# Weight sums of a seven-product FFN pair, made by adding DMA transfers, and the pair one step later

## The chip, the cores and the metric

The program runs on one core of one Trainium2 chip. The metric is the device time of one execution in microseconds (us); lower is better. TensorE (PE) multiplies, VectorE (DVE), ScalarE (ACT) and GpSimd (POOL) work on tiles in SBUF and PSUM, and SyncE (SP) issues DMA transfers. GpSimd has a DMA queue of its own.

## The reference, cut to what matters

The network works on x of 256 tokens by 1024. Around its mixers it has five feed-forward networks (FFNs), each with hidden width 2816, in float32:

```
x = x + 0.5 * swiglu(rms_norm(x, ffn1_norm_g[i]), ffn1_w_in[i], ffn1_w_out[i])

def swiglu(x, w_in, w_out):
    gate, up = jnp.split(x @ w_in, 2, axis=-1)
    return (jax.nn.silu(gate) * up) @ w_out
```

The fifth has its weights in three matrices (gate, up, down). The change touches these FFNs alone.

## The kernel before, in words

**Precision.** Each float32 operand of a product is split into a rounded part and a rest (hi and lo), and a product is three matmuls: hi by hi, hi by lo, lo by hi. For the weights ACT makes w_hi from w_raw (round_, L803) and DVE makes w_lo (split, L1412).

**Units.** The weights stream in units of 128 x 2048 float32 (1.05 MB) through a ring of three buffers. SP loads unit u when DVE has split unit u-3. PE takes a unit in 24 matmuls of 512 columns. All engines walk the same list of units.

**An FFN** has 11 steps (NI = 11), of 256 hidden columns each. G(i,0) and G(i,1) are the gate and up weights of step i for the two halves of the 1024 inputs, D(i) its down weights. PE's order is G(i,0), G(i,1), D(i-1). The hidden tile of step i goes the following way: ACT's silu and DVE's product make h_s (L895, L1527), GpSimd cuts it into 16-bit words (cut, L750), SP transposes it by DMA (turn_back, L528), GpSimd joins the words (join, L754), ACT makes y_hi (L899), DVE makes y_lo (hidden_low, L1532), and PE uses both in D(i).

**The pair.** At steps PAIR = 7 and 8 the two steps together are a 2 x 2 block product (two token halves, two input halves, two column groups). It is done with seven block products (Winograd's form of Strassen's method) and not eight, so that a pair has three units of G and four sums T1 to T4 of weight blocks in place of four units. A block product is 12 matmuls. For it:

- SP loads the four raw blocks (block, L524), half a block at a time, two halves in each of steps 1 to 4.
- DVE makes the four T sums (t_sum, L1575) in steps 3, 4 and 5.
- GpSimd makes x_sum = xg_hi + xg_lo after join(1) (x_sums, L760) and the four S sums after join(2) (s_sums, L767 to L772).
- ACT makes the hi parts (L923, L928), DVE the rests (L1581, L1587), in steps 4 to 6 and in the pair.
- In the pair PE's blocks M1, M5, M6, M2, M3, M7, M4 follow each other, and ACT and DVE combine them (snap, C11, C12, C22, C21).

GpSimd works strictly in the order written: cut(i), join(i), and in between whatever stands there.

Of the kernel before, what the change touches and what calls it, by code (L numbers as in the profile page):

```python
# [25 lines left out]
P = 128  # L26
# [17 lines left out]
PAIR = 7  # L44


def gate_at(i, half):

    if i < PAIR + 2:
        return half if i == 0 else 3 * PAIR + 1 if i == PAIR + 1 else 3 * i - 1 + half  # L50
    return 3 * i - (3 if i == PAIR + 2 else 2) + half


def down_at(i):

    if i == NI - 1:
        return 3 * NI - 2
    return 3 * i + (4 if i < PAIR - 1 else 5 if i < PAIR + 1 else 3)

# [18 lines left out]
def plan_units():  # L78

    first, opens = {}, []  # L80

    def add(name, pattern):
        first[name] = len(opens)
        opens.extend(c == "g" for c in pattern)

    ffn = "d" * (3 * NI - 1)
    add("mem", "dddd")
    add("ffn0", ffn)
    add("mixa", "ggggg" + "d" * 10)
    add("mixa_out", "d" * (A_OUT // 256))  # L90
    add("ffn1", ffn)
    add("ffn2", ffn)
    add("mixb", "d" * 7)
    add("mixb_out", "d" * (A_OUT // 256))
    add("ffn3", ffn)
# [11 lines left out]
    add("ffn4", ffn)  # L107
    return first, opens


def build(nc, a, out, known=None):
# [6 lines left out]
    with ExitStack() as ctx:  # L118
# [97 lines left out]
        t_landed = [sem(f"t_landed{k}") for k in range(4)]  # L216
        ffn_cut, ffn_back, ffn_joined = (sem(n) for n in ("ffn_cut", "ffn_back", "ffn_joined"))
# [92 lines left out]
        def bank(u):  # L310

            return 4 + (u + sum(u > U[f"ffn{f}"] + 3 * NI - 2 for f in range(5))) % RING
# [33 lines left out]
        T1, T3, T2, T4 = range(4)  # L346
        x_sum = tiles(KB(40, 8))
# [139 lines left out]
        def _(sp):  # L487
# [23 lines left out]
            def ffn(f):  # L511
                u = U[f"ffn{f}"]

                def gate_up(half, i):
                    load(u + gate_at(i, half), gu_src(f, half, i), split_cols=True)

                def down(i):
                    load(u + down_at(i), down_src(f, i))

                def block(k, half):  # L520

                    j, part = half, gu_src(f, *((0, PAIR), (0, PAIR + 1), (1, PAIR + 1), (1, PAIR))[k])[half]
                    dst = t_raw[k].rearrange("p (k c) -> p k c", k=4)[:, :, 256 * j:256 * j + 256]
                    sp.dma_start(dst, part).then_inc(t_landed[k], 16)  # L524

                def turn_back(i):
                    sp.wait_ge(ffn_cut, 2 * ((NI - 1) * nth[f] + i) + 2)
                    sp.dma_start_transpose(out=h_back, in_=h_sent).then_inc(ffn_back, 16)  # L528

# [5 lines left out]
                for i in range(1, PAIR):  # L535
                    gate_up(1, i)
                    down(i - 1)
                    if i == 1:
                        sp.wait_ge(w_used, u + 1)
                    if i < 5:  # L540
                        block(i - 1, 0)
                    gate_up(0, i + 1)
                    turn_back(i - 1)
                    if i < 5:
                        block(i - 1, 1)
                gate_up(1, PAIR)
                gate_up(1, PAIR + 1)
                down(PAIR - 1)
                turn_back(PAIR - 1)
                gate_up(0, PAIR + 2)  # L550
                gate_up(1, PAIR + 2)
                down(PAIR)
                down(PAIR + 1)
                turn_back(PAIR)
                if PAIR + 3 < NI:
                    gate_up(0, PAIR + 3)
                turn_back(PAIR + 1)
                for i in range(PAIR + 3, NI):
                    gate_up(1, i)
                    down(i - 1)  # L560
                    if i < NI - 1:
                        gate_up(0, i + 1)
                    turn_back(i - 1)
                down(NI - 1)
# [117 lines left out]
        def _(pool):  # L682
# [61 lines left out]
            def ffn(f):  # L744
# [18 lines left out]
                def s_sums():  # L763
                    a11, a12, a21, a22 = (x_sum[:, 4 * h:4 * h + 4, P * tt:P * tt + P] for tt in range(2) for h in range(2))
                    s1, s2, s3, s4 = (tiles(s_raw[:, j], P) for j in range(4))
                    pool.wait_ge(pool_done, pool_.at(f"X {f} 6"))
                    pool.tensor_tensor(s1, a21, a22, ALU.add).then_inc(pool_done, pool_(f"S1 {f}"))  # L767
                    pool.tensor_tensor(s3, a11, a21, ALU.subtract).then_inc(pool_done, pool_(f"S3 {f}"))
                    pool.wait_ge(pool_done, pool_.at(f"S1 {f}"))
                    pool.tensor_tensor(s2, s1, a11, ALU.subtract).then_inc(pool_done, pool_(f"S2 {f}"))  # L770
                    pool.wait_ge(pool_done, pool_.at(f"S2 {f}"))
                    pool.tensor_tensor(s4, a12, s2, ALU.subtract).then_inc(pool_done, pool_(f"S4 {f}"))  # L772
# [3 lines left out]
                for i in range(1, NI - 1):  # L776
                    cut(i)
                    pool.wait_ge(ffn_hl, NI * nth[f] + i)
                    join(i)
                    if i == 1:  # L780
                        x_sums()
                    if i == 2:
                        s_sums()
# [9 lines left out]
        def _(act):  # L793
# [72 lines left out]
            def ffn(f, n, gain):  # L866
                u = U[f"ffn{f}"]
# [19 lines left out]
                def silu(i, tt, src=None):  # L887
                    if src is None:
                        if tt == 0:
                            act.wait_ge(ffn_gu, (NI - 2) * nth[f] + (i + 1 if i < PAIR else i - 1))  # L890
                        else:
                            act.wait_ge(w_used, u + gate_at(i, 1) + 1)
                    if i and i + NI * nth[f]:
# [7 lines left out]
                def step(i, last=False):  # L901
                    v = u + gate_at(i, 0)
                    round_(v + 2)
                    hidden_high(i - 1, (i - 1) % 2)
                    if i == 4:
                        t_high(T1, f"T1 {f}")
                    if i == 5:
# [4 lines left out]
                    if i == 5:  # L912
                        t_high(T2, f"T2 {f}")
                    round_(v + 4)
                    if last:
                        act.wait_ge(ffn_ht, nth[f] + 1)
                        act.activation(y_hi[:, 2 * (i % 2):2 * (i % 2) + 2], tiles(ps[:, 6, :]), ACT.Copy).then_inc(ffn_hh, 1)

                def t_high(k, made):
                    act.wait_ge(vec_done, vec.at(made))  # L920
                    if k == T2:
                        act.wait_ge(pool_done, pool_.at(f"S4 {f}"))
                    act.activation(t_hi[k], t_raw[k], ACT.Copy).then_inc(act_done, act_(f"T hi {f} {k}"))  # L923

                def s_high():
                    act.wait_ge(pool_done, pool_.at(f"S4 {f}"))
# [3 lines left out]
                def taken(k, bank_):  # L930
# [2184 lines left out]
```

## Time and profile before

| what | us |
|---|---|
| runs of the kernel | 1535.16, 1537.32, 1537.65 (median 1537.32) |
| the profiled execution, its own time | 1531.57 |
| its span, first to last instruction | 1529.8 |
| PE busy in it | 1517.7 |
| DVE busy | 1094.3 |
| ACT busy | 858.6 |
| POOL busy | 358.5 |

The profile is one execution. Busy time is that in which an engine executes anything; an engine's idle time matters only where PE has to wait for it. Ends of matmuls are modelled, so waits of PE are best read from the starts of neighbouring matmuls. The mean granted clock of PE was 0.999 of full speed.

### The profile page before, as it was taken

Reading aid. Unit: us, or ns where it says so; the run is one execution under the profiler, and the core shown is the slowest. Engines: PE = TensorE matmul, PEld = TensorE weight load, DVE = VectorE, ACT = ScalarE, POOL = GpSimd, SP = SyncE. Lnnn points to the kernel's source line nnn. Section 1 sums busy time; section 2 is a strip of 40 time slices with the busy share of each in tenths; the row PEclk is TensorE's granted clock in tenths of the full one; section 3 lists DMA queues with packets and bytes.
Section 4 is the critical chain, followed back from the end, with each engine's and each line's share of the span. In section 5 each row is a group of like instructions: output and inputs, shape, how many; then the busy total and the mean of one; then the engine's idle time right before and its main releaser. Section 6 shows DMA issues by size and latency. Waiting matters only on the chain.

```text
span 1529.8 us, 19935 instructions
## 1 busy us (share of the span) xinstructions
PE 1517.7 (99%) x7906; PEld 1292.2 (84%) x7906; DVE 1094.3 (72%) x1174; ACT 858.6 (56%) x1075; POOL 358.5 (23%) x256
## 2 busy tenths in 40 slices
PE   9999999999999999999999999999999999999998
PEld 7888888888778888888888888899988899888886
DVE  6677766557778567776776678599998566666875
ACT  7545554645365454556776456476887343464554
POOL 0352200001732135320001631100571000017320
PEclk9999999999999999999999999999999999999999
DMA  7977665457776688765416986766554665578763
GB/s 253 314 243 233 188 182 188 138 170 211 239 246 192 193 275 251 228 195 173 158 56 206 285 230 203 209 191 204 181 181 147 212 192 187 173 223 273 226 194 102
DMA packets 274309, 311.43 MB, mean 204 GB/s; under 512 B 64272, under 2 KB 233512, under 8 KB 274216
## 3 DMA queue, kind: packets, MB, share of 16 engines
q1 hardware_dynamic: 273112, 308.84, 64.4%
q8 instruction: 63, 1.03, 0.3%
q10 hardware_dynamic: 1104, 1.31, 0.3%
q14 instruction: 30, 0.25, 0.0%
HBM read 295.92 MB, written 1.09 MB: 194 GB/s over the span
## 4 chain that ended last, share of the span: by engine, by line
PE 90%; POOL 3%; DVE 2%; issue 2%; DMA 2%; ACT 2%; ACTq 0%; DVEq 0%; POOLq 0%
PE ps L2344 22%; PE ps L2348 22%; PE ps L2345 22%; PE ps L2334 3%; PE ps L2336 3%; PE ps L2335 3%; PE ps L2546 2%; PE ps L2545 2%; PE ps L2544 2%; DMA scr<-scr 1%; PE ps L2387 1%; PE ps L2500 1%; POOL scr L750 1%; DVE w_lo L1412 1%; POOL scr L760 0%
## 5 line engine op out<-in xcount | busy, mean ns | idle before, releaser
L1412 DVE TENSOR_TENSOR w_lo<-w_raw,w_hi 128x2048 fp32r<-128x2048 f32 x250 | 598.5, 2400 | 185.1 <-ACT w_hi L803 184.7
L803 ACT ACTIVATE w_hi<-w_raw 128x2048 fp32r<-128x2048 f32 x250 | 477.0, 1912 | 250.8 <-PE ps L2348 200.5
L2344 PE MATMUL ps<-w_hi,xg_hi 128*128 128x512 f32 (+1 forms) x960 | 375.2, 391 | 1.2 <-DVE scr L1527 1.2
L2348 PE MATMUL ps<-w_hi,xg_lo 128*128 128x512 f32 (+1 forms) x960 | 372.1, 388 | 0.0
L2345 PE MATMUL ps<-w_lo,xg_hi 128*128 128x512 f32 (+1 forms) x960 | 372.0, 387 | 0.0
L750 POOL COPY scr<-scr 128x512 uint16<-128x512 uint16 x100 | 121.1, 1231 | 697.8 <-DVE scr L1527 697.7
L2344 PE MATMUL ps<-w_hi,y_hi 128*128 128x512 f32 x666 | 261.9, 393 | 1.3 <-DVE y_lo L1532 0.7
L2348 PE MATMUL ps<-w_hi,y_lo 128*128 128x512 f32 x666 | 259.1, 389 | 0.0
L2345 PE MATMUL ps<-w_lo,y_hi 128*128 128x512 f32 x666 | 258.9, 389 | 0.0
L2344 PEld LDWEIGHTS ps<-w_hi,xg_hi 128*128 128x128 f32 x960 | 180.3, 188 | 39.1 <-DVE w_lo L1412 1.6
L2348 PEld LDWEIGHTS ps<-w_hi,xg_lo 128*128 128x128 f32 x960 | 180.3, 188 | 36.8
L2345 PEld LDWEIGHTS ps<-w_lo,xg_hi 128*128 128x128 f32 x960 | 180.4, 188 | 36.3
L2334 PE MATMUL ps<-xg_hi,w_hi 128*128 128x256 f32 x544 | 155.1, 285 | 0.0
L2336 PE MATMUL ps<-xg_hi,w_lo 128*128 128x256 f32 x544 | 153.9, 283 | 0.0
L2335 PE MATMUL ps<-xg_lo,w_hi 128*128 128x256 f32 x544 | 153.9, 283 | 0.0
L2344 PEld LDWEIGHTS ps<-w_hi,y_hi 128*128 128x128 f32 x666 | 125.1, 188 | 28.7 <-issue 1.8
L2348 PEld LDWEIGHTS ps<-w_hi,y_lo 128*128 128x128 f32 x666 | 125.0, 188 | 26.1
L2345 PEld LDWEIGHTS ps<-w_lo,y_hi 128*128 128x128 f32 x666 | 125.2, 188 | 24.9
L754 POOL COPY scr<-scr 128x1024 uint16<-128x1024 uint16 x50 | 82.2, 1645 | 200.7 <-DMA scr<-scr 200.7
L899 ACT ACTIVATE y_hi<-scr 128x512 fp32r<-128x512 f32 x50 | 31.4, 629 | 155.0 <-POOL scr L754 154.9
L2334 PEld LDWEIGHTS ps<-xg_hi,w_hi 128*128 128x128 f32 x544 | 104.4, 192 | 0.4 <-issue 0.3
L2335 PEld LDWEIGHTS ps<-xg_lo,w_hi 128*128 128x128 f32 x544 | 104.4, 192 | 0.0
(403 smaller groups left out, 1710.8 us busy)
## 6 DMA issues: line engine op xcount, KB each, us to landing
w_raw<-in_ffn_w_in_dram SPq DMA_DIRECT2D x168, 512.0 KB, 5.0
w_raw<-in_ffn_w_out_dram SPq DMA_DIRECT2D x88, 512.0 KB, 5.5
w_raw<-in_w_in_dram SPq DMA_DIRECT2D x82, 512.0 KB, 4.6
w_raw<-in_a_w_in_dram SPq DMA_DIRECT2D x28, 512.0 KB, 4.5
w_raw<-in_w_down_dram SPq DMA_DIRECT2D x22, 512.0 KB, 5.1
w_raw<-in_w_gate_dram SPq DMA_DIRECT2D x21, 512.0 KB, 4.1
w_raw<-in_w_up_dram SPq DMA_DIRECT2D x21, 512.0 KB, 5.2
y_raw<-in_ffn_w_in_dram SPq DMA_DIRECT2D x16, 512.0 KB, 5.4
```

Source lines behind the costliest of these rows:

```text
L750: pool.tensor_copy(h_words[:, :, tt::2], h_s[:, tt].bitcast(U16).rearrange("p (b c w) -> p w b c", w=2, c=P)).then_inc(ffn_cut, 1)
L754: pool.tensor_copy(KB(20, 2).bitcast(U16).rearrange("p (b t w) -> p w b t", w=2, t=P), h_back.rearrange("p (w b) t -> p w b t", w=2)).then ...
L803: act.activation(w_hi[:, u % RING, :], w_raw[:, u % RING, :], ACT.Copy).then_inc(w_rounded, 1)
L899: act.activation(y_hi[:, 2 * p:2 * p + 2], h_t, ACT.Copy).then_inc(ffn_hh, 1)
L1412: dve.tensor_tensor(w_lo[:, s, :], w_raw[:, s, :], w_hi[:, s, :].bitcast(F32), ALU.subtract).then_inc(w_split, 1)
L2334: pe.matmul(dst, hi, xh, start=start, stop=False, skip_group_check=True)
L2335: pe.matmul(dst, hi, xl, start=False, stop=False, skip_group_check=True)
L2336: last = pe.matmul(dst, lo, xh, start=False, stop=stop, skip_group_check=True)
L2344: pe.matmul(dst, xh, hi, start=start, stop=False, skip_group_check=True)
L2345: pe.matmul(dst, xh, lo, start=False, stop=False, skip_group_check=True)
L2348: return pe.matmul(dst, xl, hi, start=False, stop=stop, skip_group_check=True)
L2544: pe.matmul(ps[:, bank_, :], xh[:, k], hi[:, c], start=start and k == 0, stop=False, skip_group_check=True)
```

## The change: what it does

- **T sums.** DVE's four subtractions go. GpSimd issues four DMA transfers, SBUF to SBUF, that add the source to what stands in the destination (add). The form of the seven products is turned so that only sums, and no differences, of weight blocks are needed: T1 += T3, T3 += T2, T2 += T1, T4 += T2. The signs move to S1 and S4 and to U2 and C22. Each transfer waits on GpSimd for the ones that it builds on.
- **Where they stand.** With p = 8 (the pair), add(T1) comes between cut(5) and join(5), add(T3) after join(5), add(T2) between cut(6) and join(6), add(T4) after join(6).
- **Sums of x.** x_sum and the S sums are made by DVE in step 5 and no longer by GpSimd in steps 1 and 2; x_sum is one instruction in place of four.
- **The pair** is at steps 8 and 9, in all five FFNs. The places of units come from a list (ffn_places), which has room for more pairs; here each FFN has one.
- **Raw blocks.** SP loads them in step 5 (T1, T3, T2) and step 6 (T4) and not in steps 1 to 4.
- **hi parts and rests.** ACT's s_high is in step 6, T1 and T2 in step 7; DVE's rests of S are in step 6, of T1 in step 7, of T2 at the head of the pair. The rest of T1 waits for add(T2), that of T2 for add(T4), since these transfers read what the rest overwrites.
- **The last hidden tile** is handled in the pair, as step 10 is now the step that follows it.

```diff
-PAIR = 7
+PAIRS_OF = ((8,), (8,), (8,), (8,), (8,))
+
+def ffn_places(pairs):
+
+    order, i = [("G", 0, 0), ("G", 0, 1)], 1
+    while i < NI:
+        if i in pairs:
+            order += [("G", i, 0), ("G", i, 1), ("G", i + 1, 1), ("D", i - 1), ("G", i + 2, 0), ("G", i + 2, 1), ("D", i), ("D", i + 1)]
+            i += 3
+        else:
+            order += [("G", i, 0), ("G", i, 1), ("D", i - 1)]
+            i += 1
+    return {step: k for k, step in enumerate(order + [("D", NI - 1)])}
...
@@ SyncE, step i (p is the pair)
+                    if i == p - 3:
+                        block(p, 0, 0)
+                        block(p, 0, 1)
+                    gate_up(1, i)
+                    if i == p - 3:
+                        block(p, 1, 0)
+                        block(p, 1, 1)
+                    down(i - 1)
+                    if i == p - 2:
+                        block(p, 3, 0)
+                    if i < NI - 1:
+                        gate_up(0, i + 1)
+                    turn_back(i - 1)
+                    if i == p - 3:
+                        block(p, 2, 0)
+                        block(p, 2, 1)
+                    if i == p - 2:
+                        block(p, 3, 1)
...
@@ GpSimd
-                def x_sums():
-                    pool.wait_ge(xl_ready, 8 * (norm_of[f"ffn{f}"][0] + 1))
-                    for k in range(0, 8, 2):
-                        pool.tensor_tensor(x_sum[:, k:k + 2], xg_hi[:, k:k + 2].bitcast(F32), xg_lo[:, k:k + 2].bitcast(F32),
-                                           ALU.add).then_inc(pool_done, pool_(f"X {f} {k}"))
...
+                def add(p, k, src):
+
+                    n = pair_count(f, p)
+                    if k in (T1, T3, T4):
+                        pool.wait_ge(t_landed[k], 32 * n)
+                    pool.wait_ge(*{T1: (t_landed[T3], 32 * n), T3: (t_landed[T2], 32 * n), T2: (t_added[T1], 16 * n), T4: (t_added[T2], 16 * n)}[k])
+                    if k == T3:
+                        pool.wait_ge(t_added[T1], 16 * n)
+                    if k == T2:
+                        pool.wait_ge(t_added[T3], 16 * n)
+                    pool.dma_start(t_raw[k], t_raw[src], accum_op=ALU.add).then_inc(t_added[k], 16)
...
                 for i in range(1, NI - 1):
                     cut(i)
+                    if i + 3 == pairs[0]:
+                        add(i + 3, T1, T3)
+                    if i + 2 == pairs[0]:
+                        add(i + 2, T2, T1)
...
                     pool.wait_ge(ffn_hl, NI * nth[f] + i)
                     join(i)
-                    if i == 1:
-                        x_sums()
-                    if i == 2:
-                        s_sums()
+                    if i + 3 == pairs[0]:
+                        add(i + 3, T3, T2)
+                    if i + 2 == pairs[0]:
+                        add(i + 2, T4, T2)
...
@@ VectorE, step i
-                    if i == 3:
-                        t_sum(T1, T3, T1, "T1")
-                    if i == 4:
-                        t_sum(T3, T2, T3, "T3")
-                    if i == 5:
-                        t_sum(T4, T4, T2, "T4")
-                    if i == 6:
-                        t_low(T2)
+                    if i == pairs[0] - 3:
+                        x_sums()
+                    if i + 2 == pairs[0]:
+                        s_lows((0, 1))
+                    if i + 1 in pairs:
+                        t_low(i + 1, T1)
                     split(v + 3)
...
+                    if i == pairs[0] - 3:
+                        s_sums()
+                    if i + 2 == pairs[0]:
+                        s_lows((2, 3))
                     split(v + 4)
...
+                def x_sums():
+
+                    dve.tensor_tensor(x_sum, xg_hi[:, :, :].bitcast(F32), xg_lo[:, :, :].bitcast(F32), ALU.add).then_inc(vec_done, vec(f"X {f}"))
...
+                def t_low(p, k):
+
+                    dve.wait_ge(act_done, act_.at(f"T hi {f} {p} {k}"))
+                    if k in (T1, T2):
+                        dve.wait_ge(t_added[T2 if k == T1 else T4], 16 * pair_count(f, p))
+                    dve.tensor_tensor(t_lo[k], t_raw[k], t_hi[k].bitcast(F32), ALU.subtract).then_inc(vec_done, vec(f"T lo {f} {p} {k}"))
...
+                def pair(p):
+
+                    n = u + at["G", p, 0]
+                    t_low(p, T2)
                     split(n + 2)
```

## Rows read from the trace of the kernel before

**Rows 1.** The page, part 1: busy us, share of the span, instructions.
```profile
PE 1517.7 (99%) x7906; PEld 1292.2 (84%) x7906; DVE 1094.3 (72%) x1174; ACT 858.6 (56%) x1075; POOL 358.5 (23%) x256
```

**Rows 2.** The waits, of PE: total us, times, longest us.
```profile
PE ps L2344 <- DVE scr L1527: 1.2, 1, 1.2
PE ps L2344 <- DVE y_lo L1532: 0.7, 1, 0.7
```

**Rows 3.** The windows, FFN 1 and FFN 2: stretch, its us, busy by engine.
```profile
372.00:522.00 150.00, 148.04 (x650) 121.43 (x649) 112.00 (x86) 76.00 (x71) 57.05 (x35) 1.00 0.76 233
522.00:701.00 179.00, 179.00 (x800) 148.26 (x799) 125.15 (x97) 94.84 (x93) 57.89 (x38) 1.00 0.73 226
```

**Rows 4.** The timeline of PE in FFN 1: start, us, instruction, idle before.
```profile
410.24 0.39 PE L2348 MATMUL ps<-w_hi,y_lo 128*128 128x512 f32 x1
411.87 0.47 PE L2344 MATMUL ps<-w_hi,xg_hi 128*128 128x512 f32 x1 [1.24 <-DVE scr L1527]
...
422.61 0.39 PE L2348 MATMUL ps<-w_hi,xg_lo 128*128 128x512 f32 x1
423.72 0.50 PE L2344 MATMUL ps<-w_hi,y_hi 128*128 128x512 f32 x1 [0.72 <-DVE y_lo L1532]
```

**Rows 5.** The timeline of POOL in FFN 1: first and last of four S sums, cuts.
```profile
400.88 3.31 POOL L767 TENSOR_TENSOR scr<-scr 128x512 f32<-128x512 f32 x1
...
409.26 3.22 POOL L772 TENSOR_TENSOR scr<-scr 128x512 f32<-128x512 f32 x1
412.43 5.30 POOL L750 COPY scr<-scr 128x512 uint16<-128x512 uint16 x2
```

**Rows 6.** The timeline of DVE in FFN 1, beside rows 5.
```profile
402.96 1.78 DVE L1532 TENSOR_TENSOR y_lo<-scr,y_hi 128x512 fp32r<-128x512 f32 x1
404.66 3.37 DVE L1575 TENSOR_TENSOR y_raw<-y_raw 128x2048 f32<-128x2048 f32 x1
407.95 3.38 DVE L1412 TENSOR_TENSOR w_lo<-w_raw,w_hi 128x2048 fp32r<-128x2048 f32 x1
```

**Rows 7.** The timeline of DVE in FFN 2, step 6.
```profile
632.27 0.69 DVE L1532 TENSOR_TENSOR y_lo<-scr,y_hi 128x512 fp32r<-128x512 f32 x1 [1.90 <-ACT y_hi L899]
632.89 2.28 DVE L1581 TENSOR_TENSOR scr_r<-scr,scr_r 128x2048 fp32r<-128x2048 f32 x1
635.09 2.28 DVE L1412 TENSOR_TENSOR w_lo<-w_raw,w_hi 128x2048 fp32r<-128x2048 f32 x1
```

**Rows 8.** The groups of instructions: count, busy us, mean ns of one.
```profile
L803 ACT ACTIVATE w_hi<-w_raw 128x2048 fp32r<-128x2048 f32 x250 | 477.0, 1912 | 250.8 <-PE ps L2348 200.5 <-PE ps L2336 40.0 <-DMA w_raw<-in_ffn_w_in_dram 7.6
...
L760 POOL TENSOR_TENSOR scr<-xg_hi,xg_lo 128x512 f32<-128x512 f32 x20 | 42.0, 2128 | 0.0
...
L1575 DVE TENSOR_TENSOR y_raw<-y_raw 128x2048 f32<-128x2048 f32 x5 | 16.9, 3377 | 0.0
...
L1575 DVE TENSOR_TENSOR scr<-scr 128x2048 f32<-128x2048 f32 x5 | 11.4, 2284 | 0.0
```

**Rows 9.** The timeline of PE in FFN 2: first matmul of D(5), of the pair.
```profile
635.96 0.39 PE L2344 MATMUL ps<-w_hi,y_hi 128*128 128x512 f32 x1
...
641.39 0.39 PE L2544 MATMUL ps<-w_hi,xg_hi 128*128 128x512 f32 x1
```

**Rows 10.** The timeline of SP in FFN 2: last raw half, turn_back(5).
```profile
596.35 0.58 SPq L524 DMA_DIRECT2D scr<-in_ffn_w_in_dram  x1
...
626.06 1.23 SPq L528 DMA_TRANSPOSE scr<-scr  x1
```

**Rows 11.** DMA issues: count, KB each, median us from issue to landing.
```profile
scr<-scr SPq DMA_TRANSPOSE x50, 3.1
...
scr<-mixer_rows SPq DMA_DIRECT2D x1, 512.0 KB, 3.6
```

**Rows 12.** The timeline of POOL in FFN 2: cut(5) and join(5).
```profile
622.80 3.23 POOL L750 COPY scr<-scr 128x512 uint16<-128x512 uint16 x2 [7.34 <-DVE scr L1527]
629.22 2.36 POOL L754 COPY scr<-scr 128x1024 uint16<-128x1024 uint16 x1 [3.18 <-DMA scr<-scr]
```

More of the change, by code:

```diff
@@ L346, in build, with pair_count, alone_until, alone @@
         T1, T3, T2, T4 = range(4)
+        def pair_count(f, p):
+            return sum(len(PAIRS_OF[g]) for g in range(f)) + PAIRS_OF[f].index(p) + 1
+        def alone_until(f, i):
+            def alone(f, j):
+                return j not in PAIRS_OF[f] and j - 1 not in PAIRS_OF[f]
+            return sum(alone(g, j) for g in range(f) for j in range(NI)) + sum(alone(f, j) for j in range(i + 1))
         x_sum = tiles(KB(40, 8))
@@ L534, in ffn @@
                     small_inputs()
-                for i in range(1, PAIR):
-                    gate_up(1, i)
-                    down(i - 1)
-                    if i == 1:
[L539 to L564, printed above, removed]
+                i = 1
+                while i < NI:
+                    if i in pairs:
+                        pair(i)
+                        i += 3
+                    else:
+                        step(i)
+                        i += 1
+                if NI - 3 not in pairs:
+                    down(NI - 1)
                 if f == 4:
@@ L911, in step @@
                         silu(i, tt)
-                    if i == 5:
-                        t_high(T2, f"T2 {f}")
+                    if i + 1 in pairs:
+                        t_high(i + 1, T2)
                     round_(v + 4)
[L915 to L923, printed above, removed]
+                    if i == NI - 1:
+                        last_hidden()
@@ L974, in ffn @@
                         act.activation(rope[:, j], rope[:, j], ACT.Sin).then_inc(act_done, act_(f"rope {j}"))
-                for i in range(3, PAIR):
-                    step(i)
-                pair()
-                for i in range(PAIR + 3, NI):
-                    step(i, last=i == NI - 1)
+                i = 3
+                while i < NI:
+                    if i in pairs:
+                        pair(i)
+                        i += 3
+                    else:
+                        step(i)
+                        i += 1
             def mem(n, gain):
@@ L1636, in ffn @@
                     pass
-                for i in range(3, PAIR):
-                    step(i)
-                pair()
-                for i in range(PAIR + 3, NI):
-                    step(i, last=i == NI - 1)
+                i = 3
+                while i < NI:
+                    if i in pairs:
+                        pair(i)
+                        i += 3
+                    else:
+                        step(i)
+                        i += 1
             def mem(n, gain, factor):
@@ L2588, in gates @@
+                    pe.wait_ge(vec_done, vec.at(f"C21 {f} {p}"))
+                    gates(p + 2)
+                    down(p)
+                    down(p + 1, hidden=(lambda: hidden(NI - 1)) if p + 2 == NI - 1 else None)
                 def gates(i, first=None):
-                    gate_up(u + gate_at(i, 0), 0, first=first)
-                    gate_up(u + gate_at(i, 1), 1)
-                for i in range(1, PAIR):
+                    gate_up(u + at["G", i, 0], 0, first=first)
+                    gate_up(u + at["G", i, 1], 1)
@@ L2594, in ffn, with step @@
+                def step(i):
                     gates(i, taken(i - 1))
@@ L2596, in ffn @@
                         pe.wait_ge(act_done, act_.at("M kT 1"))
-                    down(i - 1, start=i == 1)
-                pair()
-                for i in range(PAIR + 3, NI):
-                    gates(i, taken(i - 1))
-                    down(i - 1, hidden=(lambda: hidden(NI - 1)) if i == NI - 1 else None)
+                    down(i - 1, start=i == 1, hidden=(lambda: hidden(NI - 1)) if i == NI - 1 else None)
+                i = 1
+                while i < NI:
+                    if i in pairs:
+                        pair(i)
+                        i += 3
+                    else:
+                        step(i)
+                        i += 1
                 down(NI - 1, norm=n + 1)
```

283 lines of the change are left out of this document (152 added, 131 removed).

## The prediction

> **What bounds the kernel now.** I read the page first: TensorE (PE) is busy 1517.7 of 1529.8 us [rows 1]. The list of PE's waits has six entries, 4.8 us in all; two stand in the FFNs, 1.2 us on VectorE's (DVE's) h_s products and 0.7 us on its y_lo [rows 2]. The windows say where: the FFN stretches show PE busy all of their time but one, FFN 1, with 148.04 of 150.00 us [rows 3]. So neither the loads (DMA share about 0.75) nor DVE (125.15 of 179 us in FFN 2) binds; they only have to be in time. The change leaves PE's instructions as they are: seven products of 12 matmuls a pair, as before. All it can win is PE's waits, all it can lose is new ones.
>
> **The wait of FFN 1.** PE's timeline shows the two gaps [rows 4]. A unit is 24 matmuls, 641.39 - 635.96 = 5.43 us [rows 9], so a matmul follows its neighbour at 0.227 us. From 410.24 to 411.87 is 1.40 us too much, from 422.61 to 423.72 0.88: 2.3 us. Behind them stand GpSimd's S sums, 400.88 to 412.43, 11.6 us in one piece [rows 5]. The cuts of h_s are queued behind them and take 5.30 us (3.23 in FFN 2 [rows 12]), the transpose and the join follow them, and PE's down unit, the second gap, is late. DVE beside them needs 1.78 us for a y_lo of 0.69, 3.37 for the T1 sum and 3.38 for a split of 2.28 [rows 6, 7]; that split ends at 411.3, and PE goes on. The same sums are in the other FFNs, where 2 to 3 us of cover absorb them.
>
> The Trainium skill (SBUF — State Buffer, "Who interferes with whom") says the same of a DVE instruction with two SBUF inputs beside a GpSimd one that reads SBUF: one blocks the other. By that, moving sums off GpSimd makes both engines faster, and more than a count of instructions shows.
>
> **What is removed and added, per FFN.** GpSimd loses four x sums of 2128 ns and the S sums, 20 us in all [rows 5, 8]. DVE loses four T sums, 3.4 us the first, 2.3 the last of four [rows 8], about 10.4 us, and gains one x sum of 2048 elements (2.3 us by that last T sum) and four S sums of 512 elements (0.7 us each by y_lo [rows 7], 2.8): DVE minus 5 us. All of this is off PE. What it gives back is the 2.3 us of FFN 1, worth at most 0.15%. At pairs[0]-3 = step 5 DVE's new sums stand about where the T4 sum and T1's rest (2.5 us each) stood, so no new lateness there.
>
> The pair moves from steps 7, 8 to 8, 9: three more units in front, three fewer behind, PE's sum unchanged. The last hidden block now hangs in down(p+1) of the pair, with the same mid-unit transposes as step 10 had; down(8) now lies between gates(10) and it, so I cost it at 0.
>
> The T raw loads go from one block a step (steps 1 to 4) to three in step 5 and one in step 6. On SP's queue step 5 then puts block 0, G(5,1), block 1 and D(4) together, 4 x 1.05 MB. At 226 GB/s for a share of 0.73 the engines move 310 GB/s when busy [rows 3], so 3.4 us a megabyte. The four take 13.5 us from about 596.3, where FFN 2 issues its last raw half now [rows 10], so D(4) lands at about 610. PE takes D(5) at 635.96 [rows 9] and D(4) a step, 16.3 us, before: 619.6. ACT's rounding and DVE's split need 1.9 + 2.3 us before that [rows 7, 8], so 5 us of cover remain. Transposes turn_back(4) and (5) are issued after such bursts have drained. Cost 0.
>
> **The four adding transfers** decide. Each adds 1.05 MB of SBUF into SBUF from GpSimd's queue; before has no such operation. Bounds for one, call it L, to landing: a 0.5 MB transfer that ran by itself landed in 3.6 us [rows 11], of which 1.7 is data at 310 GB/s, so 1.9 us is fixed. One reading of 1.05 MB gives 3.4 + 1.9 = 5.3 us, the low end (no reason lets it be faster). Reading source and destination in turn gives 6.8 + 1.9 = 8.7. With half of the engines going to weight loads, 13.6 + 1.9 = 15.5, the high end. I take 8: two reads of long rows (8 KB a partition, where a weight row is 1 KB), mostly beside a weight load that has 12 us to spare.
>
> The Trainium skill (Collectives: The Full Stack, "The bandwidth ceiling") says that a DMA add costs two source reads on the reading side and so runs at half of a copy's rate. No row of before shows it. It speaks against the change: with it L is 8.7, not 5.3.
>
> Now the deadlines, with FFN 2's clock [rows 7, 9, 10, 12]. Steps are 16.3 us long, step 7 stays a step, the pair starts at 641.39 + 16.33 = 657.7.
> - T1's add is issued after cut(5), 622.80 + 3.23 = 626.0.
> - T3's waits for T1's and for join(5), 629.22 + 2.36 = 631.6: at 626 + L.
> - T2's waits for cut(6) (about 641) and T3's: max(641, 626 + 2L). join(6) is queued behind this wait.
> - T4's waits for T2's and join(6): 626 + 3L or 641 + L.
> - T2 is wanted by DVE's rest of T1, which needs 2.3 us, then a split of 2.3 [rows 7] before PE takes G(8,0) at 657.7: by 653.1, so L up to 9.0.
> - T4 is wanted by the rest of T2, which DVE now makes at the head of the pair, and PE's M6 two products later at 663.1: by 660.8, so 4L up to 34.8, L up to 8.7.
> - join(6) has to start by about 647 for D(6) at 652.3: L up to 10.5.
> At L = 8 nothing is late (T4 lands at 658). If the cover goes, each us of L over 8.7 costs 4 us a FFN, 20 us in the kernel.
>
> Sum: 2.3 us won, 0 lost. The profiled execution took 1531.57 us (span 1529.8), which would become 1529.3; the median of the three runs is 1537.3, 5.7 above it, and the result is compared with that. 1537.3 - 2.3 = **1535.0**.
>
> **Rivals.**
> *A, faster than can be overlooked.* The timed runs are 3.6 to 6.1 us longer than the profiled one. If that is the same collision, striking in more FFNs than FFN 1 (their cover of 2 to 3 us is as thin as the 5.30 us of cuts is thick), it goes too. At 1 to 1.5 us in each of the other four, 4 to 6 more are won: about 1531. For it: GpSimd's sums sit at the same place in all five. Against: no row shows such a wait outside FFN 1.
>
> *B, slower: the chain of four adds is too long.* PE waits at G(8,0) and at M6 of each pair. Point: L above 8.7 us. At L = 10, T2 lands at 656, 2.9 us late, T4 at 666, 5.2 late: 26 us, less 2.3: 1561. At L = 9.5 it is 16, so 1551; at the high end 15.5 it is 27 a FFN, 136: 1671. For it: the cover is 0.7 us by my own L, and the adds meet turn_back(5) and (6) and G(8,0)'s load. Against: the weight loads fill only 0.73 of the engines now and have slack to yield.
>
> *C, slower by little: the adds delay the transposes.* turn_back(5) is issued at 626.06 [rows 10], at the same moment as T1's add, turn_back(6) beside T2's. They land in 3.1 us now [rows 11]; y_lo for D(5) is ready at 632.27 + 0.69 = 633.0 [rows 7] and PE takes it at 635.96: 3.0 us of cover. If the transpose waits for most of one add's data (up to 6.8 us), 1 to 2 us are lost once a FFN: 5 to 10, less 2.3: about 1541. The Trainium skill (DMA: Bandwidth & Descriptors, "Queues, rings and completion order") has each DMA engine take its queues in turn, a packet at a time. If packets of an add are long, that is C; if loads get an equal share, it is B.
>
> *D, nothing is gained.* The gap in FFN 1 is made again by the x and S sums now on DVE: 1537.
>
> **Chances.** My forecast with D (within 0.2%, 3.1 us, which is about what a measurement can tell from no change): 0.38. A 0.26. B 0.26. C 0.10. The forecast's own spread puts 0.02 beyond the limit on the fast side, C puts 0.03 within it. So faster 0.28, same 0.39, slower 0.33. The range leaves out B above L = 10 (about 0.12) and the quickest of A: 1529 to 1560. The likeliest case's own range is 1533 to 1538.
>
> **What would show it.** Right: PE's waits in FFN 1's window gone; no PE wait on DVE's scr_r or y_hi rests of the T's nor on w_lo near the pair; GpSimd's cuts at 1.2 to 3.2 us; the adds landing 7 to 8.7 us after issue. B shows as DVE waiting for a DMA ahead of the rest of T1 or T2 and PE behind it, five times alike. C shows as transposes landing after 5 us and more, GpSimd's join late and PE waiting on y_lo at D(5) or D(6). The forecast is wrong above all if L is over 8.7 us, a number that nothing in this trace measures.

## The result, and the profile after

The changed kernel is slower: 1584.6 us median of four runs (1581.04 to 1586.87) against 1536.24 before, a ratio of 1.0326 with a 95% interval of 1.0307 to 1.0344. The profiled execution took 1583.5 us, with a span of 1581.7.

The page, part 1, has the same 7906 matmuls as before, and 16 us more in which PE is busy; the rest of the 52 us is idle time [rows 1].

```profile
PE 1533.7 (97%) x7906; PEld 1302.0 (82%) x7906; DVE 1052.5 (67%) x1179; ACT 860.3 (54%) x1075; POOL 261.7 (17%) x236
```

DVE lost 42 us of work and POOL 97 us. That part of the change did what it says; next to nothing of it was on the path. The waits of PE (total, times, longest) are new:

```profile
PE ps L2416 <- DVE y_lo L1594: 22.8, 4, 8.0
PE ps L2616 <- DVE scr_r L1648: 9.3, 3, 3.2
PE ps L2616 <- ACT scr L989: 6.1, 2, 3.3
```

The first is the wait for y_lo before D(5), in four FFNs of five. The other two are one place, M6 in each pair. The wait of FFN 1 behind the h_s products [rows 2] is no longer there.

The DMA issues of GpSimd's queue and the transposes (count, KB, median us to landing), and the least, median and longest landing of the adding transfers and of the transposes, from the answers for their two lines:

```profile
y_raw<-y_raw POOLq DMA_DIRECT2D x5, 1024.0 KB, 16.6
y_raw<-scr POOLq DMA_DIRECT2D x5, 1024.0 KB, 10.4
scr<-y_raw POOLq DMA_DIRECT2D x5, 1024.0 KB, 9.2
scr<-scr POOLq DMA_DIRECT2D x5, 1024.0 KB, 10.6
...
scr<-scr SPq DMA_TRANSPOSE x50, 4.6
```

```profile
DMA to landing us min/median/max: 8.6/10.4/19.1
```

```profile
DMA to landing us min/median/max: 3.0/4.6/19.3
```

In this order the four are T1, T3, T2 and T4. Three of them land in 9 to 11 us. T1's needs 16.6, and a transpose, which never took more than 8.5 us before, once takes 19.3.

FFN 2 shows why. POOL's timeline has cut(5), T1's add at 636.32, and then join(5), which waits 18.65 us for its transpose. SP's has that transpose, turn_back(5), issued at 636.39. The load behind it, which takes about 1 us to issue elsewhere, needs 11.92 here:

```profile
635.36 1.01 POOL L798 COPY scr<-scr 128x512 uint16<-128x512 uint16 x1 [1.12 <-DVE scr L1589]
636.32 0.85 POOL L817 DMA_DIRECT2D y_raw<-y_raw  x1
655.82 1.32 POOL L802 COPY scr<-scr 128x1024 uint16<-128x1024 uint16 x1 [18.65 <-DMA scr<-scr]
657.05 0.86 POOL L817 DMA_DIRECT2D y_raw<-scr  x1
...
668.01 0.86 POOL L817 DMA_DIRECT2D scr<-y_raw  x1 [1.92 <-DMA y_raw<-scr]
673.54 1.34 POOL L802 COPY scr<-scr 128x1024 uint16<-128x1024 uint16 x1 [4.67 <-DMA scr<-scr]
678.65 0.86 POOL L817 DMA_DIRECT2D scr<-scr  x1 [3.78 <-DMA scr<-y_raw]
```

```profile
636.39 1.24 SPq L548 DMA_TRANSPOSE scr<-scr  x1
637.68 1.57 SPq L544 DMA_DIRECT2D scr<-in_ffn_w_in_dram  x1
640.47 11.92 SPq L515 DMA_DIRECT2D w_raw<-in_ffn_w_in_dram  x2
...
666.12 1.44 SPq L548 DMA_TRANSPOSE scr<-scr  x1
```

Two pairs of times matter. T1's add and its transpose start 0.07 us apart, and both are held up for 19 us. T2's add starts 1.9 us behind its transpose (668.01 and 666.12), and that transpose is joined at 673.54.

PE's timeline shows both gaps of this FFN, the one before D(5) and the one before M6, and what the matmuls do behind them. Before M6 DVE waits for T4's add:

```profile
658.58 0.79 PE L2416 MATMUL ps<-w_hi,y_hi 128*128 128x512 f32 x1 [7.99 <-DVE y_lo L1594]
659.17 0.63 PE L2417 MATMUL ps<-w_lo,y_hi 128*128 128x512 f32 x1
659.60 0.63 PE L2420 MATMUL ps<-w_hi,y_lo 128*128 128x512 f32 x1
...
691.62 0.76 PE L2616 MATMUL ps<-scr_r,y_hi 128*128 128x512 f32 x1 [3.02 <-DVE scr_r L1648]
```

```profile
689.18 2.29 DVE L1648 TENSOR_TENSOR scr_r<-scr,scr_r 128x2048 fp32r<-128x2048 f32 x1 [3.26 <-DMA scr<-scr]
```

Matmuls follow each other at 0.43 us behind the gap (659.17 to 659.60), and at 0.227 elsewhere. The windows (stretch, its us, busy us by engine with counts, granted clock, DMA share, GB/s) give the clock and what the DMA engines moved:

```profile
636.00:656.00 20.00, 14.58 (x65) 11.75 (x63) 6.70 (x5) 2.50 (x2) 1.35 (x3) 0.94 1.08 114
...
648.00:652.00 4.00, 2.58 (x12) 1.81 (x10) 0.00 (x0) 0.00 (x0) 0.00 (x0) 1.00 1.50 141
652.00:656.00 4.00, 0.00 (x0) 0.00 (x0) 0.00 (x0) 0.00 (x0) 0.18 (x1) 0.71 0.72 78
656.00:660.00 4.00, 1.42 (x3) 1.16 (x4) 1.90 (x3) 2.83 (x6) 1.90 (x2) 0.50 1.11 356
660.00:664.00 4.00, 4.00 (x11) 3.11 (x10) 2.29 (x2) 4.00 (x4) 0.00 (x0) 0.51 1.13 328
664.00:668.00 4.00, 4.00 (x20) 3.29 (x19) 4.00 (x6) 1.31 (x2) 1.63 (x2) 1.00 0.96 242
```

From 656 to 664 the granted clock is 0.50, that is 1.2 and not 2.4 GHz, and PE does 11 matmuls in 4 us and not 20. It had been idle for 8 us before.

In the 20 us of the hold-up, 636 to 656, the DMA engines move 114 GB/s, where the mean over this FFN was 226 before [rows 3]: the weight loads stand too, not only the transpose. The DMA share of the same 20 us is 1.08, so the engines count as full all the time and move half as much. (A window books a packet where it starts, with all of its time, so a share can be over 1.) The trace's packet records, read one by one, say why: of the 128 packets of T1's add in this FFN 15 took over 5 us each, up to 10.9, where a packet of an add takes 0.63 us (median). In the whole kernel 21 packets are like that, all of them in the four FFNs with the hold-up.

Not every gap brings the slow clock. The trace has nine gaps of PE of 2.8 us and more, and seven of them are followed by some microseconds at half clock; the two without are one of 3.1 us and one of 3.3 us, both before M6. The window behind the first of these, which ended at 498.4:

```profile
499.00:503.00 4.00, 4.00 (x20) 3.29 (x19) 4.00 (x2) 1.62 (x2) 2.62 (x1) 1.00 0.94 281
```

### The profile page after: what moved, and what is told of

Read it like the earlier page. It is cut to its first block, busy times and chain, and to the rows that moved or that the text cites. A ratio compares the mean times of both kernels' runs of the same rounds, so it can differ in the third digit from the quotient of the medians.

```text
span 1581.7 us, 19915 instructions
## 1 busy us (share of the span) xinstructions
PE 1533.7 (97%) x7906; PEld 1302.0 (82%) x7906; DVE 1052.5 (67%) x1179; ACT 860.3 (54%) x1075; POOL 261.7 (17%) x236
## 4 chain that ended last, share of the span: by engine, by line
PE 75%; DMA 13%; DVE 5%; issue 3%; ACT 2%; POOL 2%; SPq 0%; POOLq 0%; ACTq 0%; DVEq 0%
PE ps L2416 18%; PE ps L2417 18%; PE ps L2420 18%; DMA scr<-scr 6%; PE ps L2406 3%; PE ps L2408 3%; PE ps L2407 3%; DVE w_lo L1474 2%; DMA y_raw<-scr 2%; DMA scr<-y_raw 2%; PE ps L2616 2%; PE ps L2617 2%; PE ps L2618 2%; PE ps L2459 1%; ACT w_hi L859 1%
## 5 line engine op out<-in xcount | busy, mean ns | idle before, releaser
L1474 DVE TENSOR_TENSOR w_lo<-w_raw,w_hi 128x2048 fp32r<-128x2048 f32 x250 | 584.1, 2339 | 225.6 <-ACT w_hi L859 225.3
L2416 PE MATMUL ps<-w_hi,y_hi 128*128 128x512 f32 x666 | 265.9, 399 | 23.3 <-DVE y_lo L1594 22.8
L798 POOL COPY scr<-scr 128x512 uint16<-128x512 uint16 x100 | 101.8, 1031 | 781.6 <-DVE scr L1589 781.6
L802 POOL COPY scr<-scr 128x1024 uint16<-128x1024 uint16 x50 | 78.0, 1561 | 261.3 <-DMA scr<-scr 261.3
```

Of the source, the lines that this page charges most:

```text
L798: pool.tensor_copy(h_words[:, :, tt::2], h_s[:, tt].bitcast(U16).rearrange("p (b c w) -> p w b c", w=2, c=P)).then_inc(ffn_cut, 1)
L802: pool.tensor_copy(KB(20, 2).bitcast(U16).rearrange("p (b t w) -> p w b t", w=2, t=P), h_back.rearrange("p (w b) t -> p w b t", w=2)).then ...
L1474: dve.tensor_tensor(w_lo[:, s, :], w_raw[:, s, :], w_hi[:, s, :].bitcast(F32), ALU.subtract).then_inc(w_split, 1)
L2416: pe.matmul(dst, xh, hi, start=start, stop=False, skip_group_check=True)
```

## The experiments

Theory 1: the loss comes from the adding transfers, first by the meeting of T1's add with a transpose, then by the length of the chain of four, and the slow clock behind each gap adds to both. Theory 2 in its forms puts the loss elsewhere, into the pair's place, into DVE's new sums, into the traffic as such or into any overlap. All ratios are to the kernel before, whose median was 1533.7 us in the first set of runs, 1533.8 in the second, 1534.35 in the third.

### The T sums back on VectorE

```diff
-                    if i + 3 == pairs[0]:
-                        add(i + 3, T1, T3)
...
+                    for k, src, at_ in ((T1, T3, 3), (T3, T2, 4), (T4, T2, 5)):
+                        if i == at_:
+                            t_sum(k, src)
...
+                    dve.tensor_tensor(t_raw[k], t_raw[k], t_raw[src], ALU.add).then_inc(vec_done, vec(f"T sum {f} {k}"))
```

The calls of all four adds go. Not shown in the diff: SyncE loads the raw blocks in steps 1 to 4 again, and the x sum moves from step 5 to step 3.

> The changed kernel with its four T sums back on VectorE (additions, in steps 3, 4 and 5) and the raw blocks loaded in steps 1 to 4, x sum in step 3, S sums in step 5, the pair at 8 and 9 as in the change. Theory 1 (all of the loss comes from the adding transfers, by their collision with the transposes and by the length of their chain): no PE gap above 1 us in any FFN, the clock stays at full speed, time 1533 to 1537, that is the kernel before less up to 2.3 us. Theory 2 (the pair's new place or the sums of x on VectorE cost as well): time 1540 or more, with gaps at the pair that remain.

Measured: 1529.0 us median of ten runs, ratio 0.997 (0.996 to 0.9981). In both windows, FFN 1 and FFN 2, PE is busy throughout, where FFN 1 had 148.04 of 150 us [rows 3]:

```profile
372.00:522.00 150.00, 150.00 (x665) 124.19 (x664) 112.81 (x93) 77.63 (x72) 31.94 (x27) 1.00 0.77 235
522.00:701.00 179.00, 179.00 (x801) 148.28 (x800) 128.01 (x103) 95.67 (x93) 39.88 (x30) 1.00 0.74 226
```

Theory 1 holds, and the time is below the 1533 that it gave as its low end: the loss goes with the adding transfers, and the rest of the change is worth 0.3%, 4.7 us. The raw loads moved here too, but the kernel with all adds behind joins, below, keeps them in a burst and is as fast, so it is not they. This kernel beats both.

### T1's add one step earlier, behind a join

```diff
-                    if i + 3 == pairs[0]:
-                        add(i + 3, T1, T3)
...
+                    if i + 4 == pairs[0]:
+                        add(i + 4, T1, T3)
                     if i + 3 == pairs[0]:
                         add(i + 3, T3, T2)
```

> The changed kernel with T1's adding transfer issued one step earlier, behind join(4) and not between cut(5) and join(5); all else as in the change. Theory 1 (collision: the add and the transpose turn_back(5) start within 0.1 us of each other and both then need 14 to 19 us in four FFNs of five): T1's add lands in 9 to 11 us, turn_back(5) in 3 to 5 us, the gap before D(5), 23.4 us in sum, is gone, and the time falls by 25 to 35 us (the slow clock behind the gaps goes too) to 1550 to 1560. T2's add now starts together with turn_back(6) and may collide there in its stead: then the gap moves to D(6) and the time falls by less. Theory 2 (an add is merely long, and the transposes wait for its data however they start): turn_back(5) is quick but nothing else changes, and the chain T3, T2, T4 keeps the gap before M6 at 3 us a FFN.

Measured: 1545.4 us, 1.0077 (1.0055 to 1.0099). The gaps before D(5) are gone. The waits of PE that remain are those of M6:

```profile
PE ps L2616 <- DVE scr_r L1648: 5.9, 3, 2.4
PE ps L2616 <- ACT scr L989: 5.2, 2, 2.7
```

Moving one transfer of four gives back 39.2 us by the medians, 36.8 by the spans of the two profiled executions. The pages tell how these divide, since the matmuls are the same. PE's busy time fell from 1533.7 to 1523.7, so by 10.0, and its idle time by the other 26.8:

```profile
PE 1523.7 (99%) x7906; PEld 1296.1 (84%) x7906; DVE 1053.4 (68%) x1179; ACT 860.6 (56%) x1075; POOL 262.5 (17%) x236
```

The idle time is that of the waits, 22.8 us before D(5) and 15.4 - 11.1 = 4.3 before M6, together 27. The busy time is that of the slow clock: by the trace's clock records PE was busy for 28.9 us at half clock in the change and for 10.2 here, and at half clock half of the busy time is lost, 14.5 and 5.1 us.

The feared new meeting of T2's add with turn_back(6) did not come: in FFN 2 that add is issued at 643.86 and the transpose at 642.01, 1.9 us apart as in the change, since T2's add has to wait for T3's. The time fell below the 1550 that I had as the low end. Not as expected were the landings: turn_back(5) takes 7.4 to 8.8 us and not 3 to 5, since T1's add (10.7 to 11.9 us) is still in flight when it is issued. PE has cover for that.

### All adds behind joins, one a step

The raw blocks are loaded a step earlier. The four adds stand behind join(3), join(4), join(5) and join(6).

```diff
+                    for k, src, at_ in ((T1, T3, 5), (T3, T2, 4), (T2, T1, 3), (T4, T2, 2)):
+                        if i + at_ == pairs[0]:
+                            add(pairs[0], k, src)
```

> The changed kernel with the raw blocks loaded one step earlier and the four adding transfers each behind a join, one a step: T1 behind join(3), T3 behind join(4), T2 behind join(5), T4 behind join(6). So each has about 9 us before the next transpose is issued. Theory 1 (collision and chain length explain the loss): adds land in 9 to 11 us, transposes in 3 to 5, no gap before D(5), D(6) or M6 above 1 us, PE at full clock in the FFNs, time 1533 to 1540. Theory 2 (adding transfers beside the weight stream cost by their share of the DMA engines, wherever they stand): gaps remain at weight units and the time stays above 1550.

Measured: 1530.0 us, 0.9977 (0.9966 to 0.9989). The adds are hardly quicker than in the change, T1's apart. The transposes land in 4.7 us (median), at most 9.9, and not in 3 to 5 as expected:

```profile
y_raw<-y_raw POOLq DMA_DIRECT2D x5, 1024.0 KB, 11.2
y_raw<-scr POOLq DMA_DIRECT2D x5, 1024.0 KB, 10.5
scr<-y_raw POOLq DMA_DIRECT2D x5, 1024.0 KB, 8.9
scr<-scr POOLq DMA_DIRECT2D x5, 1024.0 KB, 11.2
```

The time is below the 1533 that I had as the low end. FFN 2 has PE busy in 179.00 of 179.00 us with a DMA share of 0.87 (0.73 before). So 20 adding transfers of 9 to 13 us beside the weight stream cost nothing when they stand where nothing waits for them. Theory 2 in its form of traffic falls.

### All adds behind cuts

The same kernel, with the loop above moved up between cut(i) and join(i).

> The kernel of adds_behind_joins (0.9977 of the time before) with each of the four adding transfers moved from behind the join of its step to between cut and join of the same step, so that each is issued at the moment at which SyncE issues the transpose: four meetings a FFN where the change has one. Theory 1 (an adding transfer and a transpose that start together hold each other up): transposes of steps 3 to 6 land after up to 19 us, gaps of 3 to 8 us before many of D(3) to D(6), time 1580 to 1660. Theory 2 (the change lost by the length of the chain, not by the meeting): each add is half a step earlier than its deadline wants, so there is no gap and the time is about 1530.

Measured: 1739.4 us median of two runs, 1.134 (1.1294 to 1.1386). It is above the range that I gave. The waits of PE have one entry that matters, at all 20 places:

```profile
PE ps L2411 <- DVE y_lo L1589: 169.3, 20, 16.8
```

This is the strongest evidence for the meeting. The adds are earlier here than in the change, and only their moment is that of the transposes. The transposes at these places need 13.5 to 25.5 us and the adds 13.2 to 28.9; 103 of the adds' packets took over 5 us, and none did in the kernel with the adds behind joins. That GpSimd now issues a transfer ahead of each join is not the reason: plain copies in the same 20 places (below) cost 7.8 us.

### T1's add 3 us later, and 1.6 us earlier

In one kernel eight small fills on GpSimd stand between cut(5) and T1's add. In another the add stands between the two cuts.

```diff
+                        for k in range(8):
...
+                            pool.memset(spare[:, :], 0.0).then_inc(pool_done, pool_(f"pause {f} {k}"))
                         add(i + 3, T1, T3)
```

```diff
                 def cut(i):
                     for tt in range(2):
+                        if tt and i + 3 == PAIRS_OF[f][0]:
+                            add(i + 3, T1, T3)
```

> The changed kernel with eight small fills on GpSimd (128 x 256 float32 of a spare tile) between cut(5) and T1's adding transfer, so that it is issued 2 to 4 us behind the transpose turn_back(5) and not with it. In the change T2's add stands 1.9 us behind its transpose and lands in 9.2 us, with the transpose in 5. If it is the simultaneous start that hurts: T1's add lands in 9 to 11 us, the transpose in 3 to 5, the gaps before D(5) (23.4 us in sum) are gone, those before M6 stay or grow by a microsecond a FFN, time 1545 to 1560. If any overlap of an add with a transpose hurts: the gaps before D(5) stay, time 1580.

> The changed kernel with T1's adding transfer issued between the two cuts of step 5, so 1.5 to 2.5 us ahead of the transpose turn_back(5) and not with it; the transpose then meets an add whose data are already moving. If only the start within a fraction of a microsecond hurts: T1's add lands in 9 to 11 us, the transpose in 4 to 8, no gap above 3 us before D(5), time 1545 to 1565. If it hurts when a transpose comes upon an add that has started: the gaps before D(5) stay at 3 to 8 us or grow, time 1575 to 1600.

Measured: 1558.7 us (1.0092 to 1.0239) and 1558.8 us (1.0094 to 1.0237), both 1.0165, from two runs each. The rows of FFN 2, first the pause (POOL, then SP), then the add between the cuts (POOL, then SP):

```profile
635.16 0.86 POOL L818 DMA_DIRECT2D y_raw<-y_raw  x1 [0.18 <-issue]
635.70 1.73 POOL L803 COPY scr<-scr 128x1024 uint16<-128x1024 uint16 x1
```

```profile
632.16 1.24 SPq L549 DMA_TRANSPOSE scr<-scr  x1
```

```profile
627.67 0.85 POOL L819 DMA_DIRECT2D y_raw<-y_raw  x1
```

```profile
629.31 2.65 SPq L548 DMA_TRANSPOSE scr<-scr  x1
```

The join of the second kernel, and the largest of the waits of PE that the first one has left:

```profile
641.93 1.34 POOL L804 COPY scr<-scr 128x1024 uint16<-128x1024 uint16 x1 [12.65 <-DMA scr<-scr]
```

```profile
PE ps L2621 <- DVE w_lo L1479: 15.6, 5, 5.1
```

With the add 3.0 us behind its transpose the join could start at once. The transposes there land in 3.1 to 4.6 us, so most had all but landed when the add was issued; that run shows the meeting taken away rather than an overlap made harmless. With the add 1.6 to 2.2 us ahead, nearly all of the transpose overlaps with it: it is slow (9.4 to 12.5 us) but not stuck, and PE waits once before D(5), 1.2 us. In both kernels about 22 us of gaps are left in PE's timeline, all but 1.4 us of them at the pair: the chain of four is as late as in the change or later. In the first one, DVE stands at the rest of T1 until T2's add has landed, and the split of w_lo that PE wants is queued behind it.

So there are two effects. An overlap makes a transpose slow, by a few microseconds that the cover mostly absorbs. A start within 0.1 us can make single packets stick: an add's packets of over 5 us occur in the change (21) and behind the cuts (103), and in neither of these two kernels, where the longest packet of an add took 1.3 and 2.6 us.

### Plain copies

The four transfers without the addition, once where the change has them and once in all 20 places behind cuts.

```diff
-                    pool.dma_start(t_raw[k], t_raw[src], accum_op=ALU.add).then_inc(t_added[k], 16)
+                    pool.dma_start(t_raw[k], t_raw[src]).then_inc(t_added[k], 16)
```

> The changed kernel with the four transfers from GpSimd's queue as plain copies, SBUF to SBUF, and no additions (this leaves out the weight sums, so the products are of other weights); places, sizes and waits as in the change. Theory 1a (the length is the second reading): a packet of 8 KB takes about 315 ns and not 628, a transfer lands in 6 to 8 us, the gap before M6 is gone; if the collision comes from long packets too, turn_back(5) lands within 8 us and the time is 1535 to 1545. Theory 1b (the collision is one between GpSimd's queue and a transpose, whatever the packets do): turn_back(5) still lands after 12 us and more in most FFNs and the time stays above 1555.

> The kernel of adds_behind_cuts (1739 us, 20 meetings of an adding transfer and a transpose, 169 us of PE waits) with plain copies in place of the additions (this leaves out the weight sums). In plain_copies five such meetings cost nothing, and a transfer landed in 5 to 8 us. If the addition is needed for the hold-up: under 10 us of PE waits, time under 1550. If plain copies do it as well, only more rarely: transposes of 10 to 20 us in some of the 20 places, 20 to 80 us of waits, time 1560 to 1640.

Measured: 1535.3 us, 1.000 (0.9981 to 1.0018), as theory 1a has it, and 1544.4 us, 1.0063 (1.0045 to 1.0082). Part 3 of the pages gives the queue of GpSimd (packets, MB, share of 16 engines' span), first of the plain copies, then of the adds behind joins:

```profile
q0 software_dynamic: 2880, 20.97, 3.7%
```

```profile
q0 software_dynamic: 2880, 20.97, 6.6%
```

A copy occupies the engines for 0.037 x 1534.7 / 20 = 2.8 us, an add for 0.066 x 1531.0 / 20 = 5.05, 1.8 times as much. In the packet records one of 8 KB takes 0.628 us as an add and 0.314 as a copy. The Trainium skill says of a DMA add (Collectives: The Full Stack, "The bandwidth ceiling") that it needs two source reads and so runs at half of a copy's rate. The runs agree with the half; that a second read is the reason, none of them shows. In the change's places the copies caused one wait of PE, 4.6 us, in FFN 0, where a transpose needed 14.3 us. In all 20 places they caused 7.8 us in seven waits, against 169.3 with the adds. So plain copies are held up too, rarely and mildly. For the 20 places the first expectation is met (under 10 us of such waits, under 1550 us), though five transposes took 10.1 to 11.2 us. A copy differs from an add in the addition and in the length of its packets at once; which of the two the hold-up needs is not separated.

### The pair's place, and GpSimd's sums

Two changes to the kernel with the T sums on VectorE: the pair back at 7 and 8; or the x and S sums back on GpSimd behind join(1) and join(2).

```diff
-PAIRS_OF = ((8,), (8,), (8,), (8,), (8,))
+PAIRS_OF = ((7,), (7,), (7,), (7,), (7,))
```

```diff
+                    if i == 1:
+                        x_sums()
+                    if i == 2:
+                        s_sums()
```

> The kernel of t_sums_on_dve (0.997 of the time before) with the pair at steps 7 and 8 and not 8 and 9; x sum in step 2, S sums in step 4. If the pair's place is worth nothing, as was predicted: the same time within 0.1%, 1528 to 1531. If the 0.3% over the kernel before came from the pair's place: 1533 to 1536.

> The kernel of t_sums_on_dve with the x sums and S sums back on GpSimd, behind join(1) and join(2) as before the change; T sums on VectorE, the pair at 8 and 9. If GpSimd's sums cost the 0.3% (they hold up the cuts and VectorE beside them): the time of the kernel before, 1532 to 1536, with one or two gaps of PE around steps 3 and 4 in some FFN. If they cost nothing: 1528 to 1531 and no gaps.

Measured: 1529.9 us, 0.9974 (0.9963 to 0.9986), and 1530.7 us, 0.9982 (0.997 to 0.9994). The pair's place is worth nothing that shows. With the sums on GpSimd the gaps of FFN 1 are back [rows 4], 0.75 and 0.87 us by the starts of neighbouring matmuls:

```profile
410.54 0.47 PE L2410 MATMUL ps<-w_hi,xg_hi 128*128 128x512 f32 x1 [0.60 <-DVE scr L1590]
...
422.42 0.50 PE L2410 MATMUL ps<-w_hi,y_hi 128*128 128x512 f32 x1 [0.72 <-DVE y_lo L1595]
```

Its time lies between that of the kernel before and that with all sums on VectorE, and its interval overlaps with the latter's; it is neither the 1532 to 1536 nor the "no gaps" that were expected. The cause of the gap in FFN 1 is shown; how the 4.7 us divide between GpSimd's sums and the rest is not.

### Two pairs

```diff
-PAIRS_OF = ((8,), (8,), (8,), (8,), (8,))
+PAIRS_OF = ((4, 8), (4, 8), (4, 8), (4, 8), (4, 8))
```

> The changed kernel with two pairs in each FFN, at steps 4, 5 and 8, 9, which its lists of places allow: 12 matmuls fewer for each of five more pairs, 2.7 us each, 13.6 us in all. All adding transfers stand as the change puts them, 40 in place of 20, of which more meet a transpose. Theory 1: the gaps of the change at D(p-3) come back for both pairs, 3 to 8 us each, and the time is 1570 to 1620. If only the first pair of a FFN is hit: 1565 to 1580. If the chip rarely lets them meet: about 1540.

Measured: 1723.2 us, 1.1242 (1.1195 to 1.1288), with waits of PE of 73.8 us for y_lo and 61.3 for w_lo. The 13.6 us saved on PE are lost many times over, and this is far over my range. The waits for y_lo are the meeting again: T1's add of the first pair and its transpose start together in every FFN. Most of the waits for w_lo are not. The second pair's adds stand at other places than the expectation says (T1's behind join(5), T3's between cut(6) and join(6), T2's and T4's behind join(6)), so their chain is too late, and DVE stands at the rest of T1 with the split of w_lo behind it. FFN 1's is one of five such waits of PE of 9.9 to 12.1 us:

```profile
543.01 2.29 DVE L1648 TENSOR_TENSOR y_hi<-y_raw,scr_r 128x2048 fp32r<-128x2048 f32 x1 [13.80 <-DMA scr<-y_raw]
545.22 2.28 DVE L1474 TENSOR_TENSOR w_lo<-w_raw,w_hi 128x2048 fp32r<-128x2048 f32 x1
```

## Why the prediction was wrong, point by point

**The step that failed** is the price of rival C. The meeting was seen: turn_back(5) "at the same moment as T1's add". But it was priced as a queue that shares, a transpose that waits for most of one add's data, up to 6.8 us, 1 to 2 us a FFN, and it got a chance of 0.10. By the prediction's own terms even that sum was too low: 6.8 us of waiting less 3.0 of cover is 3.8 a FFN, 19 in all, which makes 1554 and not 1541. What happens is a hold-up of everything: the transpose, the add and the weight loads for 14 to 19 us in four FFNs of five. It cost 3 to 8 us of waits each time, 22.8 in all, and about 8 more by the clock. By the Trainium skill (DMA: Bandwidth & Descriptors, "Queues, rings and completion order") each DMA engine takes its queues in turn, a packet at a time. I estimate from that rule and from the add's 5 us on the engines, or my 6.8, that a transpose would lose at most 5 to 7 us. The trace does not agree when both start together: the transpose of FFN 2 took 19.3 us where 3.1 was the median before, and single packets took up to 10.9 us.

**L = 8 was too small.** It measured 9.2 to 10.6 us (medians of T3, T2 and T4), and 8.9 to 11.2 where nothing is stuck. The engines' part is 5 us for an add, below my 6.8, so the undersized term is the rest: 4 to 6 us and not 1.9. That number was read from a transfer on another queue. The packet records say where the rest is. In the change and in the kernel with the adds behind joins, the first packet of an add that is not stuck starts 2.3 to 4.5 us after the issue, and its packets then run for 5 to 8 us beside the weight loads.

**The deadlines were at the right place, and too strict.** The wait is at M6, by the rest of T2, by T4's add. In FFN 0, where nothing was stuck, T4's add landed 42.3 us after T1's was issued, 7.5 past my 34.8, and M6 waited 3.2: the deadline was some 4 us too early. At about 10 us I had 5.2 us a FFN; the waits are 2.8 to 3.3, 15.4 in all, and about 6 more by the clock. No run has L near 8.7, so that threshold itself is not tested; the plain copies, which take 5 to 8 us in the same places, left 0.2 us of wait at M6. This is rival B.

**The clock was left out.** No gap before was long enough to show it. Seven of the nine gaps of 2.8 us and more were followed by some microseconds at 1.2 GHz, 14.5 us lost in all; PE's busy time, 16 us longer with the same matmuls, says the same. Gaps of 2.4 to 2.7 us had it behind them too, three times in the kernel with T1's add behind a join.

Together: 22.8 before D(5), 15.4 before M6 and 14.5 of clock, less the 2.3 forecast as won, is 50.4 us. Measured are 48.4 between the medians and 51.9 between the two profiled spans.

**Right:** PE's work unchanged; the wait of FFN 1 from GpSimd's S sums, and gone with them; the pair's place at 0; the bursts of raw loads in one step at 0; DVE's new sums at 0. DVE lost 42 us where I had counted 25. Without the adding transfers the change gives 4.7 us where I had 2.3. That is rival A's size in part, and its mechanism in other FFNs was not shown.

The measured time is outside the range. Its upper end was that of B at L = 10, and C stood at about 1541. The two were never added, though both came from the same four transfers. A slower kernel had a chance of 0.33, so the direction was allowed for and the size was not.

## What to carry to other kernels

Where a transfer from GpSimd's queue is put into a chain that has DMA transposes on another queue, look at the moments of issue first: behind the join, when no transpose is in flight or due within some 8 us, the same transfers were free, and beside the transpose's issue they cost up to 17 us each. Price a hold-up by what stands behind it on that queue (here the weight loads), and allow for the slower clock behind every gap of PE of some 3 us: it took 14.5 us beside 38 us of waits here. A transfer's latency is taken from its own queue; where no trace has one, the range has to allow for more than another queue's (here 4 to 6 us beside the engines' part and not 1.9).

## What the runs showed that I had not expected

- An adding transfer of 1.05 MB, SBUF to SBUF, lands in 9 to 11 us as a rule (12.6 at most behind the joins), of which it occupies the 16 DMA engines for 5.05 us; a plain copy takes 5 to 8 as a rule and 2.8.
- An adding transfer and a transpose issued 0.07 us apart both took 19 us; with 1.6 us between them, add first, the transposes took at most 12.5; with 3.0 us, transpose first, the join found it landed. In FFN 0 of the changed kernel the two were issued 0.1 us apart and nothing was held up. Why they hold each other up, and why not always, stays open.
- While they were held up, the core's DMA engines counted as full (share 1.08) and moved 114 GB/s, half of the usual 226: packets of 0.63 us took up to 10.9.
- After PE was idle for 8 us the granted clock was 0.50 to 0.51 for another 5 us of work.
